# A new VectorE order, gates in long runs, four raw weight blocks and four gathered rows in a dense product-key expert layer

## The chip, the cores and the metric

The kernel runs on one core of a Trainium2 chip. The metric is the device time of one launch in microseconds (us), the median of the runs; lower is better.

## The reference

One inference step of a two-layer decoder for 512 prompt tokens and 8 sample tokens (520 in all, 1024 features, float32). Layer 0 mixes by a recurrence and a latent attention, layer 1 by a convolution module. After each mixer comes the expert layer that this change touches, with 128 x 128 = 16,384 experts, each one row of `u` and one row of `v`:

```python
def block(xb):
    q = (xb @ w_q).reshape(blk, PEER_HEADS, 2, PEER_HALF)          # 8 heads, 2 halves of 128
    s = jnp.einsum('thpd,phkd->thpk', q, sub_keys)
    sv, si = lax.top_k(s, PEER_TOPK)                                # 16 of 128 keys per half
    cand = sv[:, :, 0, :, None] + sv[:, :, 1, None, :]
    cand_idx = si[:, :, 0, :, None] * N_KEYS + si[:, :, 1, None, :]
    top_s, top_pos = lax.top_k(cand.reshape(...), PEER_TOPK)        # 16 experts per head and token
    idx = jnp.take_along_axis(cand_idx.reshape(...), top_pos, axis=-1)
    g = jax.nn.softmax(top_s, axis=-1)
    u, v = u_tab[idx], v_tab[idx]
    act = jax.nn.gelu(jnp.einsum('thkd,td->thk', u, xb), approximate=False)
    return jnp.einsum('thk,thkd->td', g * act, v)
```

The result is added to the scaled input and normalised. Each token picks 128 experts.

## The kernel before

The kernel computes the expert layer densely for most tokens. The experts form 128 blocks of 128. A first pass goes over the blocks of `peer_u` and computes gelu(u x) for all 520 tokens (`hidden` in the code), storing 260 KB a block in HBM (`store`). Beside it the queries are projected, the 16 best keys and pairs are found on VectorE, and for the first TD = 416 tokens a dense matrix of gates is made from one-hot products and stored in HBM by `store_gates`. The other TG = 104 tokens (96 of the prompt and the 8 samples) are gathered: their 128 picks each are fetched row by row.

The second pass, called the output pass here, goes over the 128 blocks of `peer_v`. For block m:

- SyncE loads the raw block into `u` (`load_v`, 512 KB), the hidden values of the 416 tokens into `act` (`load_hid`, 208 KB, four buffers), and for each group of 8 blocks the gates into `g` (`load_gates`, four transfers of 3, 3, 3 and 4 pieces of 128 KB, two buffers).
- ScalarE rounds the raw block to float32r (`high`, L1766, into `uh`, four buffers); it waits for the transfer and for the end of block m-4 on TensorE.
- VectorE forms the remainder (`low`, L1869, into `ul`, four buffers); that frees the raw block. It also makes the product of hidden values and gates (`gated`, L2056, one buffer), its rounded part (`ah`, L2061) and the remainder (`al`, L2063), two buffers each, so that they wait for the end of block m-2 on TensorE. All this is `gate(m, b, par)`.
- TensorE does 24 matmuls of 128x128 by 416 columns (L1731, L1732, L1733 for each of 8 chunks), accumulated in PSUM over all 128 blocks, and counts `block_done`. It waits for `ul` of the block (`split_done`) and `al` (`a_ready`).
- For the gathered tokens GpSimd (POOL) issues, one pick a block, an indirect DMA of one hidden value per token (L1605) and one of one `peer_v` row of 4 KB per token (L1612, 416 KB). They land in a ring of `RING` = 8 buffers. VectorE adds a row to `acc` by L2083 (`add_pick`), LAG = 4 blocks later, and counts `pick_done`.

VectorE's order of block m is `gate(m)`, `low(m+3)`, `add_pick(m-4)`. SyncE's order is `load_v(m+5)`, `load_hid(m+3)`, with the gates of the group after the next between them in the first four blocks of a group. All engines work their instructions in the order in which they are written, with waits on counting semaphores. `u` has two buffers, so `load_v(m)` waits until the remainder of block m-2 is made; the same buffers and waits serve `peer_u` in the first pass.

```python
def load_v(m, b):
    wait(sp, split_done, NK + m - 1)
```

The ring of rows lies over the memory of `xl`, `values` and `ranks`, which the first pass uses; so the first rows are fetched when that pass is done, all of the ring at once.

Of the kernel before, what the change touches and what calls it, by code (L numbers as in the profile page):

```python
# [20 lines left out]
F32 = mybir.dt.float32  # L21
# [7 lines left out]
P = 128  # L29
D = 1024  # L30
# [39 lines left out]
TAIL = ONES + (NP - 1) * PER_TILE + PLAIN + LAST  # L70
RING, LAG = 8, 4
STARTS = tuple(t * TT for t in range(NP)) + (TD,)
SHARES = tuple((NQ * c // 4, NQ * (c + 1) // 4) for c in range(4))
LOW = 3
LOAD = 5
AHEAD = NK
# [26 lines left out]
def wait(eng, sem, value):  # L103

    eng.wait_ge(sem, value)
    if not isinstance(value, int):
        eng.nop(nofuse=True)
# [1232 lines left out]
def peer_experts(nc, k, a, layer, xh, r):  # L1340
# [7 lines left out]
    with Stage(nc, f"experts{layer}") as s:  # L1348
        u = s.sb("u", [P, 2, KC, P])
        uh = s.sb("uh", [P, 4, KC, P], F32R)  # L1350
# [25 lines left out]

        over = Overlay(nc, s, "over_x", 4 * RING * D)
        first = over.row()
# [34 lines left out]
        gates_of = (a["gates"].rearrange("g n j i t -> (g n j i t)")[0:NG * NK * GB * TD]  # L1413
                    .rearrange("(g q j i t) -> g q j i t", g=NG, q=NQ, j=NK, i=GB))
        turn = k.ps[:, 6, 0:3 * TT].rearrange("p (c t) -> p c t", c=3)
# [12 lines left out]
        score_ready = s.sem("score_ready")  # L1428
        landed = [s.sem(f"landed{b}") for b in range(2)]
        high_done = s.sem("high_done")  # L1430
# [32 lines left out]
        with s.block() as block:  # L1463
            @block.sync
            def _(sp):
                def load(n, b):

                    wait(sp, split_done, n - 1)
                    sp.dma_start(u[:, b % 2], a["peer_u"][bass.ds(layer * NK + n, 1)]
                                 .rearrange("o p k e -> (o p) k e")).then_inc(landed[b % 2], 16)  # L1470

                def load_v(m, b):
                    wait(sp, split_done, NK + m - 1)
                    sp.dma_start(u[:, b % 2].rearrange("p k e -> p (k e)"), a["peer_v"][bass.ds(layer * NK + m, 1)]
                                 .rearrange("o e d -> (o e) d")).then_inc(landed[b % 2], 16)

# [5 lines left out]
                def store_gates(piece, par, c):  # L1482

                    n = NG // 4
                    if c == 0:
                        wait(sp, g_free, 2 * PT * piece + 2 * PT + 2)
                    sp.dma_start(gates_of[n * c:n * c + n, bass.ds(piece, 1)].rearrange("g o j i t -> (o j) g (i t)"),
                                 g[:, par, n * GB * c:n * GB * (c + 1)].rearrange("j (g i) t -> j g (i t)", i=GB)
                                 ).then_inc(g_stored[par], 16)

                def load_gates(grp, par, c):

                    q0, q1 = SHARES[c]
                    sp.dma_start(gg[:, par, q0:q1].rearrange("j q i t -> j q (i t)"),
                                 gates_of[bass.ds(grp, 1), q0:q1].rearrange("o q j i t -> (o j) q (i t)")
                                 ).then_inc(g_landed[par], 16)
# [12 lines left out]
                sp.dma_start(keys[:], a["peer_keys"][layer]).then_inc(keys_landed, 16)  # L1509
                sp.dma_start(u[:, 1], a["peer_u"][layer * NK + 1]).then_inc(landed[1], 16)  # L1510
                for n in range(2, LOAD):
                    load(n, n)
# [56 lines left out]
                def out(grp, par, b, last=False):  # L1569

                    m = GB * grp + b
                    if not last or b + LOAD < GB:
                        load_v(m + LOAD, b + LOAD)
                    if not last or b + LOW < GB:
                        load_hid(m + LOW, b + LOW)

# [25 lines left out]
            def _(pool):  # L1602
# [24 lines left out]
                for n in range(RING, P):  # L1627
                    pool.wait_ge(pick_done, n - RING + 1)
                    if n + 8 < P:
                        fetch_hidden(n + 8)  # L1630
                    fetch_row(n)
# [122 lines left out]
            def _(act_e):  # L1754
# [6 lines left out]
                def high(n, b, behind_gelu=False):  # L1761

                    act_e.wait_ge(landed[b % 2], 8 * (n - b % 2) + 16)
                    if not behind_gelu and (not isinstance(n, int) or n >= 4):
                        act_e.wait_ge(block_done, n - 3)
                    act_e.activation(uh[:, b % 4], u[:, b % 2], ACT.Copy).then_inc(high_done, 1)  # L1766

# [92 lines left out]
            def _(v):  # L1860
# [5 lines left out]
                def low(n, b):  # L1866

                    v.wait_ge(high_done, n + 1)
                    v.tensor_tensor(ul[:, b % 4], u[:, b % 2], uh[:, b % 4].bitcast(F32), ALU.subtract).then_inc(split_done, 1)  # L1869

# [176 lines left out]

                def gate(m, b, par):
                    if isinstance(m, int):
                        v.wait_ge(g_landed[par], 64 * (m // (2 * GB)) + 64)  # L2050
                    else:
                        v.wait_ge(g_landed[par], 4 * (m - GB * par - b) + 64)
                    v.wait_ge(hid_landed[b % 4], 4 * (m - b % 4) + 16)
                    if not isinstance(m, int) or m:
                        wait(v, a_ready, m)
                    v.tensor_tensor(gated[:, 0:TD].rearrange("p (q t) -> p q t", q=NQ),  # L2056
                                    act[:, b % 4, 0:TD].rearrange("p (q t) -> p q t", q=NQ),
                                    gg[:, par, 0:NQ, b], ALU.mult).then_inc(gated_ready, 1)
                    v.wait_ge(block_done, NK + m - 1)
                    wait(v, gated_ready, m + 1)  # L2060
                    v.tensor_copy(ah[:, b % 2, 0:TD], gated[:, 0:TD]).then_inc(a_high, 1)  # L2061
                    wait(v, a_high, m + 1)
                    v.tensor_tensor(al[:, b % 2, 0:TD], gated[:, 0:TD], ah[:, b % 2, 0:TD].bitcast(F32), ALU.subtract  # L2063
                                    ).then_inc(a_ready, 1)

                def add_pick(n, b):

                    if b % 8 == 0:
# [3 lines left out]
                        wait(v, weight_made, n + 8)  # L2072
                    v.wait_ge(rows_landed[b % RING], 16 * (n // RING) + 16 if isinstance(n, int) else 2 * (n - b % RING) + 16)
                    row = rows[0:TG, b % RING]
# [13 lines left out]
                def pair(i):  # L2088
                    for par in range(2):
                        for b in range(GB):  # L2090
                            m = 2 * GB * i + GB * par + b
                            gate(m, b, par)
                            if not isinstance(m, int) or m + LOW < NK:
                                low(NK + m + LOW, b + LOW)
                            if not isinstance(m, int) or m >= LAG:
                                add_pick(m - LAG, (GB * par + b - LAG) % 16)

                pair(0)
                with v.Fori(1, NG // 2 - 1) as i:
# [239 lines left out]
```

## Time and profile before

| | us |
|---|---|
| median of 3 runs | 4267.59 (4264.44 to 4269.47) |
| the profiled execution, its own time | 4264.74 |
| its span in the profile | 4262.7 |
| TensorE matmul busy | 3894.4 (91%) |
| VectorE busy | 2679.0 (63%) |
| ScalarE busy | 1169.2 (27%) |
| mean granted clock of TensorE | 0.964 |

The span is the profiled stretch of the one execution that was traced. Busy time of an engine is the time of its instructions, without waiting; matmuls are pipelined, so a busy TensorE isn't TensorE at its peak. The DMA share is the time of all packets over 16 DMA engines; packets of one engine can overlap, so that it can go above 1. A wait is idle time of an engine before an instruction, put down to what came last.

### The profile page before, as it was taken

The numbers are of one execution on the slowest core, as the hardware profiler recorded it, in microseconds if no ns is written. First come the engines' busy times: TensorE is split into PE (matmuls) and PEld (weight loads), VectorE is DVE, ScalarE is ACT, GpSimd is POOL, SyncE is SP. The second block draws the span as 40 slices with busy tenths as digits, with TensorE's granted clock in tenths as the row PEclk, the third lists the DMA queues.
The fourth block names the chain that finished last, engine by engine and source line by source line (L and its number), as shares of the span: only waits on it lengthen the run. The fifth ranks groups of instructions, "written<-read, shape, count | busy, mean of one in ns | idle before, by whom it ended". The sixth has DMA issues, their size and how long they took to land. (4 is left out here: it accounts for less than half of the span.)

```text
span 4262.7 us, 74232 instructions
## 1 busy us (share of the span) xinstructions
PE 3894.4 (91%) x26739; PEld 3653.6 (86%) x26739; DVE 2679.0 (63%) x4909; ACT 1169.2 (27%) x1585; POOL 550.9 (13%) x526
## 2 busy tenths in 40 slices
PE   8887779999999998888888987999999998898997
PEld 8763579999999997888888467999999998888886
DVE  3732256877775246777774846787777424777776
ACT  2211133233333221111113434233333321211212
POOL 0000000000000043333320000000000004333431
PEclk9888889999999999999999988999999999999999
DMA  3137323335445569999962012333554558999994
GB/s 115 50 105 249 124 84 106 119 127 184 157 159 175 187 197 252 258 262 253 258 191 69 20 40 99 107 123 132 175 178 152 184 171 212 253 265 258 268 266 132
DMA packets 342205, 715.74 MB, mean 168 GB/s; under 512 B 43681, under 2 KB 185122, under 8 KB 341666
## 3 DMA queue, kind: packets, MB, share of 16 engines
q1 hardware_dynamic: 296994, 604.61, 45.1%
q0 software_dynamic: 45056, 109.24, 10.6%
q8 instruction: 76, 1.25, 0.1%
q14 instruction: 79, 0.65, 0.1%
HBM read 584.59 MB, written 128.94 MB: 167 GB/s over the span
## 5 line engine op out<-in xcount | busy, mean ns | idle before, releaser
L1667 PE MATMUL ps<-peer_x_then_r_xh,experts_ul 128*128 128x260 f32 x4096 | 1164.2, 284 | 0.0
L1869 DVE TENSOR_TENSOR experts_ul<-experts_u,experts_uh 128x1024 fp32r<-128x1024 f32 x512 | 626.7, 1224 | 848.5 <-ACT experts_uh L1766 836.7
L1668 PE MATMUL ps<-experts_over_x_xl,experts_uh 128*128 128x260 f32 x4096 | 1154.8, 282 | 0.0
L1669 PE MATMUL ps<-peer_x_then_r_xh,experts_uh 128*128 128x260 f32 x4096 | 1153.6, 282 | 0.0
L1731 PE MATMUL ps<-experts_over_a_ah,experts_ul 128*128 128x416 f32 x2048 | 749.2, 366 | 143.7 <-DVE experts_over_a_al L2063 141.9
L1766 ACT ACTIVATE experts_uh<-experts_u 128x1024 fp32r<-128x1024 f32 x512 | 540.4, 1055 | 1081.5 <-PE ps L1733 760.7
L1667 PEld LDWEIGHTS ps<-peer_x_then_r_xh,experts_ul 128*128 128x128 f32 x4096 | 771.8, 188 | 0.0
L1669 PEld LDWEIGHTS ps<-peer_x_then_r_xh,experts_uh 128*128 128x128 f32 x4096 | 770.0, 188 | 0.0
L1668 PEld LDWEIGHTS ps<-experts_over_x_xl,experts_uh 128*128 128x128 f32 x4096 | 769.7, 188 | 0.0
L1732 PE MATMUL ps<-experts_over_a_al,experts_uh 128*128 128x416 f32 x2048 | 727.0, 355 | 0.0
L1733 PE MATMUL ps<-experts_over_a_ah,experts_uh 128*128 128x416 f32 x2048 | 726.1, 355 | 0.0
L1605 POOL DMA_INDIRECT experts_picked<-hidden,experts_h_idx x256 | 278.5, 1088 | 3216.2 <-DMA hidden<-experts_act 1337.3
L1731 PEld LDWEIGHTS ps<-experts_over_a_ah,experts_ul 128*128 128x128 f32 x2048 | 391.7, 191 | 215.1 <-DVE experts_over_a_al L2063 206.6
L1771 ACT ACTIVATE experts_act<-ps 128x520 f32<-128x520 f32 x256 | 154.9, 605 | 1007.1 <-PE ps L1669 1007.0
L1732 PEld LDWEIGHTS ps<-experts_over_a_al,experts_uh 128*128 128x128 f32 x2048 | 392.4, 192 | 2.2
L1733 PEld LDWEIGHTS ps<-experts_over_a_ah,experts_uh 128*128 128x128 f32 x2048 | 391.5, 191 | 2.7
L2083 DVE SCALAR_TENSOR_TENSOR experts_acc<-experts_over_x_rows,experts_weight,experts_acc 104x1024 f32<-104x1024 f32 x254 | 324.9, 1279 | 8.0 <-DVE experts_weight L2071 6.9
L1612 POOL DMA_INDIRECT experts_over_x_rows<-peer_v,experts_v_idx x256 | 262.0, 1023 | 137.2 <-issue 73.4
L1684 PE MATMUL ps<-experts_over_a_onei,experts_over_a_onej 128*128 128x128 f32 x1664 | 203.1, 275 | 9.6 <-DVE experts_over_a_onei L2021 9.6
L1684 PEld LDWEIGHTS ps<-experts_over_a_onei,experts_over_a_onej 128*128 128x128 f32 x1664 | 194.4, 191 | 11.2 <-issue 8.9
L1647 PE MATMUL ps<-peer_x_then_r_xh,experts_over_b_slab_l 128*128 128x260 f32 x512 | 148.6, 290 | 41.8 <-DVE experts_over_x_xl L1876 34.8
L2063 DVE TENSOR_TENSOR experts_over_a_al<-experts_over_a_gated,experts_over_a_ah 128x416 fp32r<-128x416 f32 x256 | 151.6, 592 | 22.2
(356 smaller groups left out, 4950.6 us busy)
## 6 DMA issues: line engine op xcount, KB each, us to landing
experts_u<-peer_u SPq DMA_DIRECT2D x256, 512.0 KB, 3.5
experts_u<-peer_v SPq DMA_DIRECT2D x256, 512.0 KB, 5.9
hidden<-experts_act SPq DMA_DIRECT2D x256, 260.0 KB, 2.1
gates<-experts_over_b_g SPq DMA_DIRECT2D x104, 512.0 KB, 2.9
experts_act<-hidden SPq DMA_DIRECT2D x256, 208.0 KB, 6.2
experts_over_b_g<-gates SPq DMA_DIRECT2D x96, 384.0 KB, 6.6
mla_ct<-cache SPq DMA_DIRECT2D x64, 320.0 KB, 3.9
pa_ct<-cache SPq DMA_DIRECT2D x64, 320.0 KB, 3.9
```

Source lines behind the costliest of these rows:

```text
L1605: pool.indirect_dma_start(out=picked[0:TG, n:n + 1], out_offset=None, in_=a["hidden"].rearrange("n e (t o) -> (n e t) o", o=1), in_offset= ...
L1612: pool.indirect_dma_start(out=rows[0:TG, n % RING], out_offset=None, in_=a["peer_v"].rearrange("i e d -> (i e) d"), in_offset=bass.Indirec ...
L1667: pe.matmul(o, ul[:, b % 4, c], xh[:, c, h, 0:TH], start=(c == 0), stop=False)
L1668: pe.matmul(o, uh[:, b % 4, c], xl[:, c, h, 0:TH], start=False, stop=False)
L1669: mm = pe.matmul(o, uh[:, b % 4, c], xh[:, c, h, 0:TH], start=False, stop=(c == KC - 1))
L1684: mm = pe.matmul(k.ps[:, 4 + m, e * NK:(e + 1) * NK], onej[:, b % 2, 4 * m + e], onei[:, b % 2, 4 * m + e], start=True, stop=True)
L1731: pe.matmul(o, ul[:, b % 4, c], ah[:, b % 2, 0:TD], start=first, stop=False)
L1732: pe.matmul(o, uh[:, b % 4, c], al[:, b % 2, 0:TD], start=False, stop=False)
L1733: mm = pe.matmul(o, uh[:, b % 4, c], ah[:, b % 2, 0:TD], start=False, stop=last)
L1766: act_e.activation(uh[:, b % 4], u[:, b % 2], ACT.Copy).then_inc(high_done, 1)
L1869: v.tensor_tensor(ul[:, b % 4], u[:, b % 2], uh[:, b % 4].bitcast(F32), ALU.subtract).then_inc(split_done, 1)
L2083: v.scalar_tensor_tensor(acc[0:TG], row, w, acc[0:TG], ALU.mult, ALU.add).then_inc(pick_done, 1)
```

## The change

- `u` has four buffers in place of two. `load` and `load_v` wait for the remainder of the block four before, and run LOAD = 7 blocks ahead in place of 5. The first four `peer_u` blocks are asked for at the start.
- The gates lie in HBM as (group, j, piece, i, t) in place of (group, piece, j, i, t). A load now reads, for each of the 128 partitions, one run of 3 or 4 KB in place of 3 or 4 runs of 1 KB; a store still writes runs of 1 KB, which now lie 13 KB apart.
- VectorE's `gate` is cut into `product` (L2056) and `split` (L2061 and L2063). Its order of block m is now `split(m)`, `low(m+2)`, `add_pick(m-4)`, `product(m+1)`.
- SyncE issues `load_hid` ahead of `load_v`.
- `RING` is 4 in place of 8: four rows in the ring, and the hidden values of the picks are asked for after the pick that is four before the row, not eight.

```diff
-RING, LAG = 8, 4
+RING, LAG = 4, 4
-LOAD = 5
+LOAD = 7
...
-        u = s.sb("u", [P, 2, KC, P])
+        u = s.sb("u", [P, 4, KC, P])
...
-        over = Overlay(nc, s, "over_x", 4 * RING * D)
+        over = Overlay(nc, s, "over_x", 4 * KC * 2 * TW + 8 * NT * HP * TOPK)
...
-                    .rearrange("(g q j i t) -> g q j i t", g=NG, q=NQ, j=NK, i=GB))
+                    .rearrange("(g j q i t) -> g j q i t", g=NG, q=NQ, j=NK, i=GB))
...
                 def load_v(m, b):
-                    wait(sp, split_done, NK + m - 1)
-                    sp.dma_start(u[:, b % 2].rearrange("p k e -> p (k e)"), ...
-                                 ).then_inc(landed[b % 2], 16)
+                    wait(sp, split_done, NK + m - 3)
+                    sp.dma_start(u[:, b % 4].rearrange("p k e -> p (k e)"), ...
+                                 ).then_inc(landed[b % 4], 16)
...
-                    sp.dma_start(gates_of[n * c:n * c + n, bass.ds(piece, 1)].rearrange("g o j i t -> (o j) g (i t)"),
+                    sp.dma_start(gates_of[n * c:n * c + n, :, bass.ds(piece, 1)].rearrange("g j o i t -> j g (o i t)"),
...
-                    sp.dma_start(gg[:, par, q0:q1].rearrange("j q i t -> j q (i t)"),
-                                 gates_of[bass.ds(grp, 1), q0:q1].rearrange("o q j i t -> (o j) q (i t)")
+                    sp.dma_start(gg[:, par, q0:q1].rearrange("j q i t -> j (q i t)"),
+                                 gates_of[bass.ds(grp, 1), :, q0:q1].rearrange("o j q i t -> (o j) (q i t)")
...
-                sp.dma_start(u[:, 1], a["peer_u"][layer * NK + 1]).then_inc(landed[1], 16)
-                for n in range(2, LOAD):
+                for n in range(1, 4):
+                    sp.dma_start(u[:, n], a["peer_u"][layer * NK + n]).then_inc(landed[n], 16)
+                for n in range(4, LOAD):
                     load(n, n)
...
                     m = GB * grp + b
+                    if not last or b + LOW < GB:
+                        load_hid(m + LOW, b + LOW)
                     if not last or b + LOAD < GB:
                         load_v(m + LOAD, b + LOAD)
-                    if not last or b + LOW < GB:
-                        load_hid(m + LOW, b + LOW)
...
                     pool.wait_ge(pick_done, n - RING + 1)
-                    if n + 8 < P:
+                    if 16 <= n + 8 < P:
                         fetch_hidden(n + 8)
...
-                def gate(m, b, par):
+                def product(m, b, par):
...
                                     gg[:, par, 0:NQ, b], ALU.mult).then_inc(gated_ready, 1)
+
+                def split(m, b):
                     v.wait_ge(block_done, NK + m - 1)
                     wait(v, gated_ready, m + 1)
...
-                            gate(m, b, par)
-                            if not isinstance(m, int) or m + LOW < NK:
-                                low(NK + m + LOW, b + LOW)
+                            split(m, b)
+                            if not isinstance(m, int) or 0 < m < NK + 1 - LOW:
+                                low(NK + m + LOW - 1, b + LOW - 1)
                             if not isinstance(m, int) or m >= LAG:
                                 add_pick(m - LAG, (GB * par + b - LAG) % 16)
+                            if not isinstance(m, int) or m + 1 < NK:
+                                product(m + 1, (b + 1) % GB, (GB * par + b + 1) // GB % 2)
+
+                product(0, 0, 0)
                 pair(0)
```

## Rows read from the trace of the kernel before

**Rows 1.** Windows of the output pass: busy us (and instructions) by engine, PEclk, DMA share, GB/s.
```profile
...
1560.00:1650.00 90.00, 73.46 (x349) 69.43 (x350) 58.51 (x77) 15.37 (x15) 46.69 (x41) 0.92 0.95 249
1650.00:2150.00 500.00, 446.65 (x2238) 417.46 (x2237) 364.45 (x479) 98.48 (x93) 191.29 (x187) 0.99 0.96 256
3650.00:4150.00 500.00, 454.33 (x2292) 424.18 (x2291) 373.23 (x490) 100.60 (x95) 195.81 (x191) 0.99 0.96 262
...
```

**Rows 2.** The same windows, instructions of line L1731 (TensorE) alone.
```profile
...
1560.00:1650.00 90.00, 44.19 (x117) 23.73 (x117) 0.92 0.95 249
1650.00:2150.00 500.00, 272.03 (x746) 141.69 (x745) 0.99 0.96 256
3650.00:4150.00 500.00, 277.47 (x764) 144.14 (x764) 0.99 0.96 262
...
```

**Rows 3.** Waits in 1650:2150: who for whom, total us, times, longest.
```profile
...
ACT experts_uh L1766 <- PE ps L1733: 251.5, 62, 5.6
ACT experts_uh L1766 <- DMA experts_u<-peer_v: 149.4, 31, 7.8
...
PE ps L1731 <- DVE experts_over_a_al L2063: 53.0, 67, 3.1
...
```

**Rows 4.** Timeline of one block and a half: ScalarE, then VectorE, then TensorE.
```profile
...
1673.97 1.06 ACT L1766 ACTIVATE experts_uh<-experts_u 128x1024 fp32r<-128x1024 f32 x1 [3.46 <-PE ps L1733]
...
1684.09 1.06 ACT L1766 ACTIVATE experts_uh<-experts_u 128x1024 fp32r<-128x1024 f32 x1 [3.55 <-PE ps L1733]
...
1675.06 1.23 DVE L1869 TENSOR_TENSOR experts_ul<-experts_u,experts_uh 128x1024 fp32r<-128x1024 f32 x1 [0.42 <-ACT experts_uh L1766]
1676.20 1.28 DVE L2083 SCALAR_TENSOR_TENSOR experts_acc<-experts_over_x_rows,experts_weight,experts_acc 104x1024 f32<-104x1024 f32 x1
...
1678.56 0.59 DVE L2063 TENSOR_TENSOR experts_over_a_al<-experts_over_a_gated,experts_over_a_ah 128x416 fp32r<-128x416 f32 x1
...
1674.99 0.35 PE L1732 MATMUL ps<-experts_over_a_al,experts_uh 128*128 128x416 f32 x1
...
1679.10 0.35 PE L1733 MATMUL ps<-experts_over_a_ah,experts_uh 128*128 128x416 f32 x1
...
```

**Rows 5.** DMA issues in 1650:2150: count, KB each, median us from issue to landing.
```profile
...
DMA packets 63222, 128.24 MB, mean 256 GB/s; under 512 B 10480, under 2 KB 41583, under 8 KB 63217
...
experts_u<-peer_v SPq DMA_DIRECT2D x93, 512.0 KB, 6.2
experts_act<-hidden SPq DMA_DIRECT2D x94, 208.0 KB, 6.5
...
experts_over_b_g<-gates SPq DMA_DIRECT2D x11, 512.0 KB, 11.0
...
experts_over_x_rows<-peer_v,experts_v_idx POOLq DMA_INDIRECT x93, 7.9
```

**Rows 6.** DMA issues in 1000:1500, the hidden stretch, same columns.
```profile
...
experts_u<-peer_u SPq DMA_DIRECT2D x74, 512.0 KB, 3.6
...
experts_over_b_g<-gates SPq DMA_DIRECT2D x2, 512.0 KB, 3.8
```

**Rows 7.** 10 us windows with DMA share 1.03 or more: first, lowest, highest, last of 36.
```profile
...
1650.00:1660.00 10.00, 8.79 (x47) 8.35 (x46) 5.82 (x10) 1.69 (x2) 4.08 (x4) 1.00 1.05 259
...
1950.00:1960.00 10.00, 8.35 (x44) 7.63 (x42) 7.17 (x11) 1.06 (x1) 2.87 (x3) 1.00 1.04 230
...
2070.00:2080.00 10.00, 9.34 (x48) 8.84 (x48) 7.72 (x11) 2.04 (x3) 4.09 (x4) 1.00 1.05 303
...
4110.00:4120.00 10.00, 9.15 (x49) 8.76 (x48) 7.79 (x10) 2.11 (x2) 4.05 (x5) 1.00 1.03 286
...
```

**Rows 8.** Windows of the hidden stretch and of the pass's start in layer 1.
```profile
...
1100.00:1200.00 100.00, 100.00 (x850) 99.81 (x848) 72.08 (x96) 36.13 (x51) 0.00 (x0) 1.00 0.57 189
...
3560.00:3600.00 40.00, 33.50 (x162) 31.91 (x161) 22.91 (x32) 6.35 (x7) 31.02 (x26) 0.91 1.05 239
...
```

**Rows 9.** Waits of the whole span: ScalarE's for the gate stores.
```profile
...
ACT experts_over_b_g L1783 <- DMA gates<-experts_over_b_g: 35.4, 12, 3.8
...
```

More of the change, by code:

```diff
@@ L1428, in peer_experts @@
         score_ready = s.sem("score_ready")
-        landed = [s.sem(f"landed{b}") for b in range(2)]
+        landed = [s.sem(f"landed{b}") for b in range(4)]
         high_done = s.sem("high_done")
@@ L1466, in load @@
                 def load(n, b):
-                    wait(sp, split_done, n - 1)
-                    sp.dma_start(u[:, b % 2], a["peer_u"][bass.ds(layer * NK + n, 1)]
-                                 .rearrange("o p k e -> (o p) k e")).then_inc(landed[b % 2], 16)
+                    wait(sp, split_done, n - 3)
+                    sp.dma_start(u[:, b % 4], a["peer_u"][bass.ds(layer * NK + n, 1)]
+                                 .rearrange("o p k e -> (o p) k e")).then_inc(landed[b % 4], 16)
                 def load_v(m, b):
-                    wait(sp, split_done, NK + m - 1)
-                    sp.dma_start(u[:, b % 2].rearrange("p k e -> p (k e)"), a["peer_v"][bass.ds(layer * NK + m, 1)]
-                                 .rearrange("o e d -> (o e) d")).then_inc(landed[b % 2], 16)
+                    wait(sp, split_done, NK + m - 3)
+                    sp.dma_start(u[:, b % 4].rearrange("p k e -> p (k e)"), a["peer_v"][bass.ds(layer * NK + m, 1)]
+                                 .rearrange("o e d -> (o e) d")).then_inc(landed[b % 4], 16)
                 def store(n, b):
@@ L1761, in high @@
                 def high(n, b, behind_gelu=False):
-                    act_e.wait_ge(landed[b % 2], 8 * (n - b % 2) + 16)
+                    act_e.wait_ge(landed[b % 4], 4 * (n - b % 4) + 16)
                     if not behind_gelu and (not isinstance(n, int) or n >= 4):
                         act_e.wait_ge(block_done, n - 3)
-                    act_e.activation(uh[:, b % 4], u[:, b % 2], ACT.Copy).then_inc(high_done, 1)
+                    act_e.activation(uh[:, b % 4], u[:, b % 4], ACT.Copy).then_inc(high_done, 1)
                 def gelu(n, b):
@@ L1868, in low @@
                     v.wait_ge(high_done, n + 1)
-                    v.tensor_tensor(ul[:, b % 4], u[:, b % 2], uh[:, b % 4].bitcast(F32), ALU.subtract).then_inc(split_done, 1)
+                    v.tensor_tensor(ul[:, b % 4], u[:, b % 4], uh[:, b % 4].bitcast(F32), ALU.subtract).then_inc(split_done, 1)
                 v.memset(q[:, :, T:NT * TT], 0.0).then_inc(q_cleared, 1)
@@ L2072, in add_pick @@
                         wait(v, weight_made, n + 8)
-                    v.wait_ge(rows_landed[b % RING], 16 * (n // RING) + 16 if isinstance(n, int) else 2 * (n - b % RING) + 16)
+                    v.wait_ge(rows_landed[b % RING], 16 * (n // RING) + 16 if isinstance(n, int) else 16 // RING * (n - b % RING) + 16)
                     row = rows[0:TG, b % RING]
```

## The prediction

> **What bounds the kernel now.** I read the windows first, to see which stretch has room. In the stretches where the hidden values of the experts are computed TensorE is busy all the time (1100 to 1200 us: 100.00 of 100 us) and the DMA engines 0.57 of it [rows 8]; no edit here shortens TensorE's own work, so the diff can gain nothing there. In the output pass (some 690 us in each layer, from 1536 and from 3540 us) TensorE is busy 446.65 and 454.33 of 500 us while the DMA share is 0.96 [rows 1]. This pass is where the change works.
>
> Its pace: a block has 8 matmuls of L1731. 746 of them in 500 us are 93.25 blocks, 5.36 us each; in layer 1, 764 are 95.5 blocks, 5.24 us each [rows 2]. Mean 5.30. What TensorE needs: two matmuls 22 apart start at 1674.99 and 1679.10 us, so one takes 0.187 us and a block of 24 takes 4.49 us [rows 4]. So 0.81 us of each block is lost.
>
> Who makes it wait: in the chain of waits TensorE waits for al (67 times, 53.0 us), al is late because VectorE stood before ul, and ul waits for ScalarE's uh. ScalarE waited 62 times for TensorE (251.5 us) and 31 times for peer_v (149.4 us) [rows 3]. These are two different causes:
>
> First a loop through three engines. high(m+3) may overwrite uh only when block m-1 is done; it starts at 1673.97, then low at 1675.06, the pick at 1676.20, then the product and the cast, and al at 1678.56, which ends at 1679.15: 5.18 us [rows 4]. That frees block m+1, which runs 4.49 us. 9.67 us and the hand-overs make the 10.12 us from that ScalarE activation (1673.97) to the next but one (1684.09): two blocks, 5.06 us each. The loop holds the pace even when every transfer is in time.
>
> Second late transfers. load_v(m+5) is issued after low(m+3), some 2.3 us after TensorE ended block m-1 (1.06 of high, 1.23 of low [rows 4]), and is due when it ends block m+1. That leaves 10.1 - 2.3 = 7.8 us, where the median from issue to landing is 6.2 [rows 5], so the slower ones are late. These are the stalls between 5.06 and 5.30.
>
> **The change part by part.** *VectorE's order.* The same five operations a block, 4.09 us from the start of low to the end of al [rows 4], with a start-up gap some 4.2. Now split(m) comes first and needs only block m-2 done; al is ready about 1.2 us after that, and is needed 4.49 us after it. low(m+2) needs high(m+2), which waits for the same block m-2 and runs beside the split. Low, pick and product end about 4.2 to 4.3 us after it, before block m-1 ends. The 5.06 us loop is gone, and VectorE's own limit, 4.2 to 4.4, lies just under 4.49. Behind the product's wait for hid and gates now stand the next split, low and pick; the split has 3.3 us to spare. Without that cover a late hid costs its whole delay.
>
> *Four raw blocks.* The issue of load_v(m+7) hangs on low(m+3), as load_v(m+5) did, but is due two blocks later: 7.8 us of slack become about 18. It costs no instruction. In the ring of SyncE, load_hid is now issued ahead of load_v; it has about 11 us until its product, against a median landing of 6.5 [rows 5]. The hidden stretches have both the DMA room and a busy TensorE [rows 8], so early u blocks are worth nothing there; I take 0 (at most a few us at each start).
>
> *So the DMA engines are the next limit.* A block moves 512 KB of peer_v, 208 of hidden, 208 of gates and 416 of gathered rows; 128.24 MB over 93.25 blocks is 1.375 MB [rows 2, 5]. What can they give when they never run dry? From one side: of the 100 windows of 10 us in 1650:2150 and 3650:4150, 36 have a share of 1.03 or more (packets overlap, so it passes 1), with a mean of 274 GB/s, lowest 230 [rows 7]. That is 5.01 us a block. From the other side: the engine time of a block is 0.96 x 5.30 = 5.09 us [rows 1, 2]; at the 1.045 that the full windows show, 4.87 us. The first picks out the windows heavy in gathered rows, the second takes packets to grow no slower under load. I take 4.94, the middle.
>
> *Gates in long runs.* Loads of 1 KB runs become runs of 3 to 4 KB. In the uncrowded stretch 512 KB of gates take 3.8 us to land where 512 KB of peer_u take 3.6: 5%. In the output pass it is 11.0 against 6.2 for peer_v, 44% [rows 5, 6]. At 257 GB/s 208 KB are 0.83 us, so the bounds are 0.04 and 0.36 us a block; part of the 11.0 is the queue ahead of it, so I take the nearer 0.04: 4.90 us. A loss is not excluded either: 128 write runs of the store now lie 13 KB apart. Stores land in the stretch with free DMA and the two buffers of g hide them; I take 0, and at most the 35.4 us that ScalarE waits for stores today could double [rows 9].
>
> *Four gathered rows.* A row is asked for after the pick four earlier, not eight: POOL takes about 2.4 us to issue the pair, then 7.9 median to land [rows 5], against four blocks, 19.6 us. Hidden, and only a landing over 17 us would show. At the start four rows fewer, 1.70 MB, go ahead of the first peer_v blocks, in a window of 249 GB/s where a block takes 90 / (117 / 8) = 6.2 us [rows 1, 2]: 6.8 us a layer. Two more blocks are loaded before the pass, where the DMA has room: 1.05 MB, 4 us. That is 0 to 22 us in both layers; rows put off come back as load, so I take 13.
>
> Sum: from 1650 us to the last loads some 102 blocks a layer, 204 x (5.30 - 4.90) = 82 us, and 13: 95. The profiled execution took 4264.7 us (span 4262.7), so 4170; the median of the runs is 2.9 above that execution, so **4173 us**.
>
> One page of the Trainium skill makes another case of it. The rows show 1.04 of share with 274 GB/s. DMA: Bandwidth & Descriptors, "Where 436 GB/s comes from", gives some 358 GB/s as what HBM lets a core have, and more when it is alone. At 358, 1.375 MB would be 3.8 us and TensorE's 4.49 the bound, as in the second rival. In this pass the trace does not agree: no full 10 us window passes 303.
>
> The opposite is in HBM Reference, "Latency": an access takes 0.2 us on average and 2 us at high load. By that, more loads under way buy waiting and not rate, as in the third and the last rival. The trace agrees in part: peer_u lands in 3.6 us in the quiet stretch and peer_v in 6.2 here.
>
> **The rivals.** *Forecast, 0.52:* the DMA engines set 4.8 to 5.0 us, 4150 to 4195.
>
> *TensorE becomes the bound, 0.18.* If the contention between gathered rows and the rest eases once both are spread evenly, or long runs bring the 0.36, the pace is 4.6 with the clock's dips: 204 x 0.70 = 143, and the some 29 blocks of the two starts (2 x 117 / 8) go from 6.2 to about 5.1, 32 us. 175 us: 4093. At 4.49 throughout, 204 x 0.81 + 32 = 197: 4070. For it: 303 GB/s in one window would carry 4.54. Against: share 0.96 already.
>
> *Only a part comes, 0.16.* The rate does not rise above today's in full windows of layer 0, 270 GB/s, and late hid or gates take the place of late peer_v: 5.1 to 5.2 us. 204 x 0.15 = 31: about 4237.
>
> *Nothing, 0.06.* The loop was a shadow of a DMA bound that holds today: 5.30 stays, 4268.
>
> *Slower, 0.08: rate lost to more transfers at once.* When eight rows and the peer_v loads go together at the start of layer 1, the share is 1.05 and only 239 GB/s move [rows 8]. With four raw blocks always under way that could be the lasting state: 1.375 / 0.239 = 5.75 us, 204 x 0.45 = 92 us more, 4360. It decides below 1.375 / 5.30 = 259 GB/s. For it: 23 full windows of layer 0 lie only 12 GB/s above that on the mean. Against: the rows come one a block either way, and the start has eight of them at once.
>
> **How the numbers follow.** The likeliest case gives 4173. The slower side of the part case ends near 4245, the TensorE case reaches to about 4080; this range leaves out the no-change and slower cases (0.14) and the far edge of TensorE's (0.04). What this kernel's measurement can tell from no change is about 0.2%, 8.5 us. Faster 0.86, same 0.06, slower 0.08.
>
> **What would show it.** ScalarE's waits for peer_v nearly vanish (31 in layer 0's 500 us); about 102 blocks (816 of L1731) in 1650:2150 in place of 93.25; DMA share above 1.00 in most 10 us windows, at 265 to 285 GB/s; VectorE waits at the product for hidden or gates, or at the split for TensorE. TensorE idle next to a DMA share under 0.95 would mean a new wait, hid first, then rows. A rate under 259 at a share of 1.04 would make the prediction wrong in sign; TensorE busy all through at over 290 GB/s, wrong in size.

## The result, and the profile after

The changed kernel takes 4231.38 us in the median (4227.86 to 4243.52), the kernel before 4266.01 us in the runs beside it. The ratio is 0.9924, 95% interval [0.9905, 0.9943]: 0.76% faster, some 32 us where 95 were forecast. The time lies in the stated range, near the value of the third case ("only a part comes", 4237). The profiled execution took 4235.68 us, with a span of 4233.6.

TensorE's matmuls of the output pass run from 1531.7 to 2204.9 us and from 3520.5 to 4193.8 us: 673.2 and 673.3 us, where they took 689.7 (1536.4 to 2226.1) and 683.9 us (3540.3 to 4224.2). That is 27 us of the 29 by which the two spans differ.

The windows of the pass after, as in [rows 1] (busy us and instructions of TensorE, its weight loads, VectorE, ScalarE, POOL; clock, DMA share, GB/s), and under them those of L1732 alone, which is L1731 of before:

```profile
...
1560.00:1650.00 90.00, 80.21 (x396) 77.31 (x396) 66.31 (x89) 17.32 (x17) 47.88 (x37) 0.94 0.97 263
1650.00:2150.00 500.00, 450.75 (x2279) 435.18 (x2278) 366.97 (x485) 101.40 (x96) 223.42 (x190) 0.97 1.00 260
3650.00:4150.00 500.00, 448.43 (x2257) 433.22 (x2256) 364.76 (x482) 99.57 (x94) 227.52 (x188) 0.96 0.99 260
...
1560.00:1650.00 90.00, 48.55 (x132) 26.13 (x132) 0.94 0.97 263
1650.00:2150.00 500.00, 275.19 (x760) 146.72 (x760) 0.97 1.00 260
3650.00:4150.00 500.00, 273.59 (x753) 146.06 (x752) 0.96 0.99 260
...
```

760 and 753 of L1732 are 95.0 and 94.1 blocks in 500 us: 5.26 and 5.31 us a block, mean 5.29, against 5.30 before [rows 2]. The steady pace did not move; 102 blocks were forecast. The DMA share rose from 0.96 to 1.00 and 0.99, but the rate stayed at 260 GB/s (256 and 262 before).

Only the start of the pass is better. These are the first 90 us of the pass in each layer, the same line alone, before and after:

```profile
...
1536.40:1626.40 90.00, 45.24 (x120) 24.16 (x120) 0.92 0.87 227
3540.30:3630.30 90.00, 45.07 (x117) 24.19 (x117) 0.89 0.88 222
...
1531.70:1621.70 90.00, 49.88 (x139) 26.42 (x139) 0.98 0.88 236
3520.50:3610.50 90.00, 50.10 (x138) 26.80 (x139) 0.96 0.86 235
...
```

That is 19 and 21 matmuls of this line more, 5 blocks in both layers; at 5.3 us a block they are 26 of the 27 us.

The chain of waits in 1650:2150 (who for whom: total us, times, longest), as [rows 3]:

```profile
...
ACT experts_uh L1767 <- PE ps L1734: 408.5, 96, 11.3
...
DVE experts_over_a_gated L2057 <- issue: 54.3, 28, 4.9
DVE experts_over_a_gated L2057 <- DMA experts_act<-hidden: 52.5, 24, 5.3
PE ps L1732 <- DVE experts_over_a_al L2066: 48.9, 29, 5.0
...
```

ScalarE's 31 waits for peer_v are gone. In their place VectorE waits 52 times at the product, 24 times with the hidden values named, for 106.8 us in all; where "issue" is named, the profile shows no releaser. TensorE waits 29 times for 48.9 us, where it waited 67 times for 53.0: fewer and longer stalls, the same sum. DMA issues (count, KB each, median us to landing), as [rows 5]:

```profile
...
DMA packets 50534, 130.01 MB, mean 260 GB/s; under 512 B 10537, under 2 KB 22545, under 8 KB 50530
...
experts_u<-peer_v SPq DMA_DIRECT2D x94, 512.0 KB, 9.4
experts_act<-hidden SPq DMA_DIRECT2D x94, 208.0 KB, 11.7
...
experts_over_x_rows<-peer_v,experts_v_idx POOLq DMA_INDIRECT x95, 10.4
```

peer_v lands after 9.4 us in place of 6.2, the hidden values after 11.7 in place of 6.5: more is under way at the same rate, so everything is under way longer. The 11.7 us are more than the 11 us that the prediction gave load_hid.

Between stalls the new order does what it should. ScalarE's activations of three blocks in a row (start, length, line, what ended the idle time):

```profile
...
1672.04 1.06 ACT L1767 ACTIVATE experts_uh<-experts_u 128x1024 fp32r<-128x1024 f32 x1 [3.42 <-PE ps L1734]
1676.58 1.06 ACT L1767 ACTIVATE experts_uh<-experts_u 128x1024 fp32r<-128x1024 f32 x1 [3.48 <-PE ps L1734]
1681.00 1.06 ACT L1767 ACTIVATE experts_uh<-experts_u 128x1024 fp32r<-128x1024 f32 x1 [3.36 <-PE ps L1734]
1685.47 1.06 ACT L1767 ACTIVATE experts_uh<-experts_u 128x1024 fp32r<-128x1024 f32 x1 [3.42 <-PE ps L1734]
1692.21 1.06 ACT L1767 ACTIVATE experts_uh<-experts_u 128x1024 fp32r<-128x1024 f32 x1 [5.68 <-PE ps L1734]
...
```

1685.47 - 1672.04 is 13.43 us for three blocks, 4.48 each, TensorE's own pace; the fourth takes 6.74, the stall. So the kernel has a fast pace and stops for data. The question is why the DMA engines, at a share of 1.00, move no more than 260 GB/s.

### The profile page after: what moved, and what is told of

Read it like the earlier page. It is cut to its first block and busy times, and to the rows that moved or that the text cites. A ratio compares the mean times of both kernels' runs of the same rounds, so it can differ in the third digit from the quotient of the medians.

```text
span 4233.6 us, 74185 instructions
## 1 busy us (share of the span) xinstructions
PE 3878.6 (92%) x26739; PEld 3673.4 (87%) x26739; DVE 2674.5 (63%) x4909; ACT 1171.3 (28%) x1585; POOL 630.8 (15%) x526
## 5 line engine op out<-in xcount | busy, mean ns | idle before, releaser
L1732 PE MATMUL ps<-experts_over_a_ah,experts_ul 128*128 128x416 f32 x2048 | 743.3, 363 | 130.4 <-DVE experts_over_a_al L2066 130.0
L1732 PEld LDWEIGHTS ps<-experts_over_a_ah,experts_ul 128*128 128x128 f32 x2048 | 396.8, 194 | 163.8 <-DVE experts_over_a_al L2066 159.3
L1613 POOL DMA_INDIRECT experts_over_x_rows<-peer_v,experts_v_idx x256 | 342.4, 1337 | 121.4 <-issue 73.6
L2057 DVE TENSOR_TENSOR experts_over_a_gated<-experts_act,experts_over_b_g 128x416 f32<-128x416 f32 x256 | 150.9, 589 | 264.5 <-DMA experts_act<-hidden 134.1
```

Of the source, the lines that this page charges most:

```text
L1613: pool.indirect_dma_start(out=rows[0:TG, n % RING], out_offset=None, in_=a["peer_v"].rearrange("i e d -> (i e) d"), in_offset=bass.Indirec ...
L1732: pe.matmul(o, ul[:, b % 4, c], ah[:, b % 2, 0:TD], start=first, stop=False)
```

## The experiments

In each table of this section the ratio is to the kernel before, run on the same chip, with its 95% interval; blocks are the matmuls of `ah` with `ul` (L1731 before, L1732 after) in 1650:2050 over 8 (before 599 / 8 = 74.9, after 615 / 8 = 76.9), and GB/s is that window's rate (258 and 261).

### What in the transfers sets the rate

Three theories: 1, a ceiling on bytes at 260 GB/s; 2, the gathered rows slow the rest (by their scattered addresses, by the software queue, or otherwise); 3, there is rate to spare and only the hidden values stand in the wrong place.

`e1_rows_plain_pool` replaces the gather:

```diff
-                    pool.indirect_dma_start(
-                        out=rows[0:TG, n % RING], out_offset=None, in_=a["peer_v"].rearrange("i e d -> (i e) d"),
-                        in_offset=bass.IndirectOffsetOnAxis(ap=v_idx[0:TG, n:n + 1], axis=0),
-                    ).then_inc(rows_landed[n % RING], 16)
+                    pool.dma_start(rows[0:TG, n % RING], a["peer_v"][layer * NK + n, 0:TG]).then_inc(rows_landed[n % RING], 16)
```

> The changed kernel, but the 104 rows of a pick are 104 neighbouring rows of peer_v, loaded by a plain transfer on GpSimd's queue: same bytes, same software queue, no scattered addresses (the picked rows are replaced, so the gathered tokens get other rows). Theory 1, a ceiling on bytes (the pass moves about 260 GB/s whatever the transfers are): the pace of a block stays at 5.28 us, the time within 10 us of the changed kernel. Theory 2, scattered rows are what is slow: rate 290 to 330 GB/s, pace 4.6 to 4.8 us, 120 to 170 us faster. Theory 3, hidden values come late because they stand behind peer_v in SyncE's ring: no change, as in theory 1, but with DMA share left over.

`e2_rows_plain_sync` has the same plain rows in SyncE's `out`, behind `load_v`:

```diff
...
+                    sp.dma_start(rows[0:TG, b % RING], a["peer_v"][bass.ds(layer * NK + m, 1), 0:TG].rearrange("o e d -> (o e) d")
+                                 ).then_inc(rows_landed[b % RING], 16)
...
```

> As the run before, but the plain rows are issued on SyncE's queue after load_v, so that in the pass the software queue carries only the 4-byte hidden values (rows replaced as there). Theory 1: pace 5.28 us, rate 260 GB/s still. Theory 2, if it is the second queue and not the addresses that slows the packets: rate 300 or more, pace at TensorE's 4.5 to 4.7 us, 150 us faster. Theory 3: one more transfer a block ahead of the hidden values in the same ring, so slower, 5.4 us or more.

`e3_no_gate_loads` puts a count in place of the transfer in `refill`:

```diff
-                    load_gates(grp + 2, par, c)
+                    sp.sem_inc(g_landed[par], 16)
```

> The changed kernel without the gate loads after the first two groups of a layer (the gates of the first two groups are used again): 1.163 MB a block in place of 1.376. Theory 1: 1.163 MB at 260 GB/s is 4.47 us, so TensorE's 4.49 us becomes the bound, pace 4.5 to 4.65 us, 160 to 190 us faster, DMA share about 0.95. Theory 2: the rows and what runs beside them cost what they did, 4.5 to 4.7 us as well. Theory 3: hidden values still stand behind four peer_v blocks, pace 5.0 to 5.2 us, at most 60 us faster.

`e4_64_gathered` is the one line `TD = 448`.

> The changed kernel with TD = 448 in place of 416, which is 64 gathered prompt tokens in place of 96: 72 rows in place of 104 a pick (288 KB), hidden and gates 224 KB each, 1.278 MB a block; TensorE's block is 448/416 of 4.49, 4.83 us; some 18 us more for the gate matmuls of 32 more tokens in both layers. Theory 1: 1.278 MB at 260 GB/s is 4.92 us, 92 us less and 18 more: 4155 to 4165 us. Theory 2: fewer rows lift the rate too, TensorE is the bound at 4.85 to 4.9 us: 4140 to 4150 us. Theory 3: 5.2 us, about 4240 us.

| run | us | ratio | blocks | GB/s |
|---|---|---|---|---|
| e1_rows_plain_pool | 4120.70 | 0.9651 [0.9622, 0.9680] | 82.8 | 286 |
| e2_rows_plain_sync | 4229.77 | 0.9898 [0.9847, 0.9950] | 74.8 | 255 |
| e3_no_gate_loads | 4139.08 | 0.9692 [0.9662, 0.9722] | 81.6 | 238 |
| e4_64_gathered | 4162.42 | 0.9755 [0.9722, 0.9787] | 82.0 | 262 |

Theory 3 falls with e3: without the gate loads, 15% fewer bytes, the kernel is 92 us faster than the changed one, where theory 3 allowed 60. Theory 1 falls too: the same bytes in e1 move at 286 GB/s, and in e3, with the rows' part of the bytes larger, at 238; its pace is 400 / 81.6 = 4.90 us where a ceiling of 260 GB/s gave 4.5 to 4.65. So the rows are suspect. e4 with fewer of them came out as theory 1 said (4155 to 4165), but does not tell the two apart: its pace is 400 / 82.0 = 4.88 us and TensorE's block there is 4.83. Theory 2 in the forms asked for doesn't fit either: e3 is slower than the 4.5 to 4.7 us it gave, and away from the software queue (e2) the rows were as slow as before.

### The addresses, or the number of rows

`g1_indirect_neighbours` leaves the indirect transfers and overwrites their list:

```diff
-                v.tensor_scalar(v_idx[:], pair_of[:], float(layer * NK * P), None, ALU.add)
+                v.tensor_scalar(number[:], k.iota[:], float(P), token[:], ALU.mult, ALU.add).then_inc(idx_made, 1)
+                v.wait_ge(idx_made, 3)
+                v.tensor_scalar(v_idx[:], number[:], float(layer * NK * P), None, ALU.add)
...
```

> The changed kernel with its indirect transfers of rows as they are, but the list of addresses is overwritten by 104 neighbouring rows of peer_v a pick (so other rows than the picked ones are added). Theory 2a, scattered addresses are what costs: as with plain rows on GpSimd's queue, pace 4.8 to 4.85 us, 284 to 290 GB/s, about 4120 us. Theory 2b, the indirect form of transfer costs (how its 104 descriptors are made and spread over the engines): pace stays at 5.2 to 5.3 us, about 4230 us.

`g2_112_rows` gathers eight rows more, which no one reads:

```diff
-                        out=rows[0:TG, n % RING], ...
-                        in_offset=bass.IndirectOffsetOnAxis(ap=v_idx[0:TG, n:n + 1], axis=0),
+                        out=rows[0:112, n % RING], ...
+                        in_offset=bass.IndirectOffsetOnAxis(ap=v_idx[0:112, n:n + 1], axis=0),
```

> The changed kernel, gathering 112 rows a pick in place of 104 (the last 8 are not used; 104 isn't divisible by 16, 112 is). Theory 2a, scattered rows cost by their number: 8% more rows, pace 5.35 to 5.45 us, 15 to 35 us slower than the changed kernel. Theory 2c, 104 rows are spread unevenly over the 16 DMA engines and that costs the rate: share and rate rise, pace under 5.1 us, 40 us or more faster.

`s4_128_rows` and `q3_120_rows` are the same edit with 128 and 120, `r1_96_rows` with 96 after the first four picks, and `r2_128_plain_sync` is e2 with 128 plain rows.

> The changed kernel, gathering 128 rows a pick (the last 24 unused): 1.474 MB a block in place of 1.376, but 8 rows for each of 16 engines. If the even spread is what 112 rows brought: the engines give some 309 GB/s, 4.77 us a block, 4105 to 4140 us, faster than 104 rows although 7% more bytes move. If the busiest engine counts alone (8 rows either way, as with 13 engines of 8 rows): 4230 us or more.

> The changed kernel, gathering 120 rows a pick (120 = 15 x 8). Theory 4 in its exact form, the number of engines that take part is the largest divisor up to 16: 15 engines of 8 rows, between 104 (13 of 8, 4231 us) and 128 (16 of 8, 4055 us): 4060 to 4130 us. If only a multiple of 16 matters: 4240 us or more, by the 15% more rows.

> The changed kernel, gathering 96 rows (16 x 6) a pick after the first four picks (the 8 sample tokens keep the rows of the first four, so their result is left out). 120 rows were no faster than 104, so sharing by a divisor up to 16 is not all of it. If a multiple of 16 is what counts, 96 are at least as fast as 128: 4045 to 4070 us. If each engine must write its own 8 partitions (128 fits, 112 nearly, 96 least), rows stay slow: 4120 us or more, slower than 112 rows though fewer bytes.

> As e2_rows_plain_sync (plain rows on SyncE's queue, other rows than the picked ones) but 128 rows of it in place of 104. If the row count alone made that run slow: as fast as 128 gathered rows, 4050 to 4070 us. If plain rows on SyncE's queue are slow for another reason (one ring for all): 4230 us or more, with 7% more bytes.

| run | rows | us | ratio | blocks | GB/s |
|---|---|---|---|---|---|
| r1_96_rows | 96 | 4054.99 | 0.9490 [0.9463, 0.9518] | 88.3 | 296 |
| g1_indirect_neighbours | 104 | 4235.53 | 0.9914 [0.9890, 0.9939] | 75.8 | 258 |
| g2_112_rows | 112 | 4067.03 | 0.9541 [0.9507, 0.9576] | 87.8 | 309 |
| q3_120_rows | 120 | 4239.10 | 0.9936 [0.9911, 0.9960] | 74.9 | 267 |
| s4_128_rows | 128 | 4055.13 | 0.9498 [0.9478, 0.9518] | 88.5 | 326 |
| r2_128_plain_sync | 128, plain | 4037.64 | 0.9449 [0.9422, 0.9476] | 88.6 | 327 |

Neighbouring addresses in the same indirect transfer change nothing (4235.53). Eight rows more make the kernel 164 us faster than the changed one. The 128-row kernels came out faster than was expected of them. Windows in 1650:2050, one row each of 104 rows (after), 112, 120 and 128:

```profile
...
1650.00:2050.00 400.00, 363.76 (x1846) 352.32 (x1845) 295.40 (x389) 82.33 (x78) 181.42 (x154) 0.97 1.00 261
...
1650.00:2050.00 400.00, 396.70 (x2106) 393.44 (x2105) 340.26 (x449) 92.94 (x88) 211.21 (x175) 1.00 1.02 309
...
1650.00:2050.00 400.00, 359.52 (x1795) 349.62 (x1794) 291.23 (x383) 78.48 (x74) 182.28 (x150) 0.94 1.00 267
...
1650.00:2050.00 400.00, 400.00 (x2125) 397.63 (x2125) 346.64 (x455) 94.29 (x89) 196.37 (x178) 1.00 0.92 326
...
```

The two shares of 1.00 in the uneven cases stand for 261 and 267 GB/s; with 128 rows a share of 0.92 stands for 326, and TensorE is busy 400.00 of 400 us. TensorE's granted clock (0.97 after, 1.00 with 128 rows) is 3% apart and cannot make paces of 5.20 and 4.52 us a block, 15% apart. The DMA issues of the same four (packets and rate, peer_v, rows):

```profile
...
DMA packets 40643, 104.44 MB, mean 261 GB/s; under 512 B 8492, under 2 KB 18173, under 8 KB 40640
...
experts_u<-peer_v SPq DMA_DIRECT2D x76, 512.0 KB, 9.1
...
experts_over_x_rows<-peer_v,experts_v_idx POOLq DMA_INDIRECT x77, 10.3
...
DMA packets 45590, 123.72 MB, mean 309 GB/s; under 512 B 7698, under 2 KB 18902, under 8 KB 45586
...
experts_u<-peer_v SPq DMA_DIRECT2D x88, 512.0 KB, 6.5
...
experts_over_x_rows<-peer_v,experts_v_idx POOLq DMA_INDIRECT x88, 8.1
...
DMA packets 39720, 106.96 MB, mean 267 GB/s; under 512 B 7114, under 2 KB 16620, under 8 KB 39717
...
experts_u<-peer_v SPq DMA_DIRECT2D x75, 512.0 KB, 8.9
...
experts_over_x_rows<-peer_v,experts_v_idx POOLq DMA_INDIRECT x75, 10.6
...
DMA packets 47376, 130.43 MB, mean 326 GB/s; under 512 B 7784, under 2 KB 19093, under 8 KB 47372
...
experts_u<-peer_v SPq DMA_DIRECT2D x88, 512.0 KB, 5.2
...
experts_over_x_rows<-peer_v,experts_v_idx POOLq DMA_INDIRECT x89, 6.2
```

With 128 rows both the rows and peer_v, which nobody touched, land in little more than half the time of after, though a row transfer is 23% larger. SyncE's queue (hardware_dynamic in the profile) carries the same transfers a block in all of these kernels. Packets, MB and the share of 16 engines that its packets took, with 104, 112 and 128 rows:

```profile
...
q1 hardware_dynamic: 27278, 72.02, 65.7%
...
q1 hardware_dynamic: 31546, 83.30, 65.6%
...
q1 hardware_dynamic: 31767, 83.83, 58.0%
...
```

Over 76.9, 87.8 and 88.5 blocks these are 3.42, 2.99 and 2.62 us of engine time a block for the same bytes: the other transfers' packets last longer beside 104 rows, at a full share too (after and 112).

96, 112 and 128 rows are fast, 104 and 120 slow. What separates the five is that the number of partitions is a multiple of 16. 120 rows were expected to lie between 104 and 128 if only the number of engines that take part mattered; they were as slow as 104. r1 speaks against each engine having to write its own eight partitions. r2 shows the same on the other queue: e2 was slow by its 104 rows, and 128 rows there are the fastest run of all.

Two runs limit the rule. The 72 rows of e4 are no multiple of 16 either, and its TensorE was busy 399.02 of 400 us: it needed only 262 GB/s, so it can't show whether 72 rows are slow. And the transfers of one hidden value a token kept their 104 partitions in every run of the table, the fast ones too; with 4 bytes a partition they did not hold the rate down.

The Trainium skill, DMA: Bandwidth & Descriptors, "Why a DMA increments its semaphore by 16 and not by 1", says that a transfer runs on the largest number of engines up to 16 that divides the slowest dimension of both its sides, here the rows, and names one exception: the software queue spreads some plain transfers over all 16, the partitions over 16 rounded up on each. By that, 96, 112 and 128 rows run on 16, 104 on 13 and 120 on 15, and e1, if it is such an exception, puts 7 rows on an engine and fills 15. The split into fast and slow agrees with it. e1's 104 rows (286 GB/s) lie between the gathered 104 (261) and 112 (309), yet gathered rows on 15 engines (q3) gave 267. So the time does not follow from counting engines, and the page doesn't say why 15 cost as much as 13.

### What the parts of the change are worth

With 104 rows: `p1_gates_short` undoes the layout of the gates, `q1_104_rows_old_order` and `q2_104_rows_two_raw` undo the order and the raw blocks, `p2_before_ring4` is the kernel before with the ring alone. With 112 rows: `s1_before_112_rows`, `s2_112_rows_old_order`, `s3_112_rows_two_raw`. The edits of order and raw blocks are those of the diff of the change, taken back; their main lines:

```diff
-                            split(m, b)
-                            if not isinstance(m, int) or 0 < m < NK + 1 - LOW:
-                                low(NK + m + LOW - 1, b + LOW - 1)
+                            product(m, b, par)
+                            split(m, b)
+                            if not isinstance(m, int) or m + LOW < NK:
+                                low(NK + m + LOW, b + LOW)
...
-                            if not isinstance(m, int) or m + 1 < NK:
-                                product(m + 1, (b + 1) % GB, (GB * par + b + 1) // GB % 2)
-
-                product(0, 0, 0)
...
```

```diff
-LOAD = 7
+LOAD = 5
...
-        u = s.sb("u", [P, 4, KC, P])
+        u = s.sb("u", [P, 2, KC, P])
...
-                    wait(sp, split_done, NK + m - 3)
+                    wait(sp, split_done, NK + m - 1)
...
```

> The changed kernel with the layout of the gates of before (loads in 1 KB runs). If the runs are worth what the prediction took, 0.04 us a block, 8 to 10 us slower than the changed kernel, about 4240 us; if engine time sets the pace (a packet of 1 KB costs more for its bytes than one of 3 KB), up to 0.36 us a block and 4300 us; under a bound by scattered rows no change, 4230 us.

> The kernel before with only the ring of rows cut from 8 to 4. If the gain of the change lies in the starts of the two passes and comes from the four rows that no longer go ahead of the first peer_v blocks: 10 to 14 us a layer faster than before, about 4240 us. If it comes from the four raw blocks or the order: no change, 4266 us. If the ring of 8 hid late rows: slower than before.

> The changed kernel (104 rows) with VectorE's order of before. If the 35 us of the change come from the order: 4260 to 4270 us. Theory 4, the uneven rows hold both orders at 5.2 to 5.3 us a block and the loop of 5.06 is covered by them: within 10 us of 4231 us.

> The changed kernel (104 rows) with two raw blocks and LOAD 5. If the four raw blocks brought the 35 us, since under a slow rate the late peer_v blocks need the longer lead: 4255 to 4270 us. If the order brought them, with peer_v late but nothing queued behind it on VectorE that TensorE needs at once: 4230 to 4240 us.

> The kernel before, gathering 112 rows a pick in place of 104. Theory 4: today both kernels are held by the uneven spread of 104 rows over the DMA engines; with that gone the kernel before meets its next limit, the loop of high, low, pick, product and split with TensorE, 5.06 us a block: passes of some 650 us, 4190 to 4215 us. If the loop were no limit of its own: as fast as the changed kernel with 112 rows, 4067 us.

> The changed kernel with 112 rows and VectorE's order of before (product, split, low(m+3), pick), everything else as changed. Theory 4: the loop is back, 5.06 us a block where transfers are in time, 4185 to 4205 us. If the order is worth nothing: 4067 us.

> The changed kernel with 112 rows and two raw weight blocks (LOAD 5) in place of four, VectorE's new order kept. A peer_v block has some 6.9 us between its issue and its need, against a landing of 6.5 us median: late about every other time, pace 4.7 to 4.9 us, 4100 to 4150 us. If the raw blocks are worth nothing: 4067 us.

| run | us | ratio | blocks | GB/s |
|---|---|---|---|---|
| p1_gates_short | 4231.46 | 0.9917 [0.9886, 0.9948] | 76.1 | 260 |
| p2_before_ring4 | 4284.10 | 1.0033 [1.0012, 1.0054] | 73.5 | 253 |
| q1_104_rows_old_order | 4298.48 | 1.0070 [1.0050, 1.0090] | 71.9 | 247 |
| q2_104_rows_two_raw | 4230.62 | 0.9916 [0.9898, 0.9933] | 75.6 | 259 |
| s1_before_112_rows | 4209.05 | 0.9867 [0.9844, 0.9889] | 78.0 | 274 |
| s2_112_rows_old_order | 4180.03 | 0.9794 [0.9772, 0.9817] | 78.6 | 278 |
| s3_112_rows_two_raw | 4087.14 | 0.9581 [0.9554, 0.9609] | 87.3 | 307 |

With even rows the loop of the prediction comes out. The kernel before with 112 rows paces 400 / 78.0 = 5.13 us and the changed one with the old order 400 / 78.6 = 5.09, where the loop was put at 5.06; with the new order it is 4.56 (g2). What waits in s2 and in s3:

```profile
...
ACT experts_uh L1767 <- PE ps L1734: 319.3, 79, 5.0
...
DVE experts_ul L1870 <- ACT experts_uh L1767: 75.3, 69, 1.9
...
PE ps L1732 <- DVE experts_over_a_al L2066: 34.7, 39, 1.2
...
ACT experts_uh L1767 <- DMA experts_u<-peer_v: 268.8, 75, 6.7
...
PE ps L1732 <- DVE experts_over_a_al L2066: 4.9, 6, 1.1
```

In s2 no wait for a transfer is left, and TensorE still waits 39 times for al: the loop by itself. In s3 ScalarE waits 75 times for peer_v, but in the new order nothing that TensorE needs at once stands behind it, and TensorE waits six times for 4.9 us. So the late peer_v blocks, which the prediction took for a cause of their own, cost little once the order is new: 20 us between s3 and g2, nothing with 104 rows (q2 is level with the changed kernel). s3 came out faster than was expected of it; q1 fell outside both of its expectations on the slow side.

## Why the prediction was right in its case for a gain and wrong in its size

The step that failed is "So the DMA engines are the next limit". It read the share of 0.96 as room: 274 GB/s from full windows, 4.87 us from engine time, and between them 4.94 us a block. But with 104 rows the transfers already held the pace near 5.3 us: 112 rows alone make the kernel before 1.3% faster (s1). Measured: the share of 1.00 and 0.99 in the two layers, mean 0.995, times 5.29 is 5.26 us of engine time a block, where 5.09 was held fixed; the packets of a block took 3% longer in all. So the share rose without the rate. Full windows were no measure of the rate either: of the changed kernel's in 1650:2150 the fastest and the slowest with a share of 1.03 or more are

```profile
...
1920.00:1930.00 10.00, 10.00 (x55) 9.94 (x54) 7.30 (x10) 2.12 (x2) 3.12 (x4) 1.00 1.05 298
...
2120.00:2130.00 10.00, 8.71 (x45) 7.97 (x43) 5.79 (x8) 1.27 (x3) 3.93 (x4) 1.00 1.03 222
...
```

and the mean over 500 us is still 260. The time of a packet is no measure of what the engines could do: with 128 rows a block of 7% more bytes took 0.92 x 4.52 = 4.16 us of engine time. The 82 us of the steady stretch were 204 x (5.30 - 5.29) = 2, and the 13 us of the two starts were some 26. That 104 rows set this limit is shown by g2, s4 and r1; by what mechanism uneven rows do it stays open.

Point by point, the rest:

- **The loop** of 5.06 us a block was real, but the rows' limit lay over it, at 5.3. Freed from them it measured 5.13 (s1) and 5.09 (s2). With 104 rows the order is worth more than the whole change: without it the changed kernel is 0.7% slower than before, with it 0.76% faster. In that run (q1) the pace is 400 / 71.9 = 5.56 us at 247 GB/s and a share of 1.01, and peer_v lands after 13.9 us; why was not tried further.
- **VectorE's limit** of 4.2 to 4.4 us under TensorE's 4.49 held: with 128 rows TensorE never stops and the pace is 400 / 88.5 = 4.52.
- **Four raw blocks**: the waits for peer_v vanished, as forecast, and the time didn't change; the stalls moved to the product and its hidden values, which were named as the next to be late. With two raw blocks and the new order (q2) peer_v lands after 6.8 us at 259 GB/s, with four (after, same window) after 9.1 at 261: the longer landing is the queue, not a slower rate.
- **Long gates**: 0.04 us a block was taken; nothing measurable (4231.46 against 4231.38), and no loss from the stores.
- **Four rows in the ring**: no late rows in the steady stretch, as forecast. The ring does bring the start: in 1560:1650 the line has 117 matmuls before, 129 with the ring alone (p2), 131 without the new order (q1), 130 without the raw blocks (q2) and 132 with everything. So the 13 us of the sum were too small, not too large. But alone the ring makes the kernel 0.33% slower, since the steady stretch has 588 matmuls in 400 us against 599. The 1.70 MB a layer that are put off are some 6.5 us at 260 GB/s; that they explain it was not shown.
- **The rivals**: "only a part comes" hit the time (4237 against 4231) by luck. It had the late hidden values and the unchanged rate right, but its 31 us were to come from a steady pace of 5.1 to 5.2 us, which stayed at 5.29, while the starts brought what it did not count. For the steady stretch the rival given 0.06, "nothing", was right: a bound by the DMA that held before too. The low rate of the last rival (239 GB/s) did not become the lasting state, but q1 comes close to it: four raw blocks with the old order, 247 GB/s, below the 259 that it named, and slower than before. TensorE as the bound was right about the kernel and wrong about this change: it needed eight more rows. The Trainium skill's 358 GB/s (DMA: Bandwidth & Descriptors, "Where 436 GB/s comes from") is not contradicted after all: 327 GB/s were reached at a share of 0.91 with TensorE the bound (r2), and one window of 10 us with 128 rows (s4, 1910:1920) shows 401. The Trainium skill's statement that HBM accesses take longer at high load (HBM Reference, "Latency") agrees with landings that grew from 6.2 to 9.4 us at the same rate with more loads under way, but load by itself is not the cause: with 128 rows more bytes move and peer_v lands after 5.2.

The version to keep is the changed kernel with 128 gathered rows, the result unchanged: 4055.13 us, 5.0% faster than before.

## What to carry to other kernels

A DMA share near 1 says that packets are under way all the time, not that the engines give what they can; compare the rate with that of another stretch or shape before taking it for the limit. Where a large transfer, gathered or plain, has a number of partitions that 16 does not divide, try one that it does, padded with rows that nobody reads: 23% more bytes in the gather were 176 us faster. And a part of a change is worth something only against the limit that binds: the same new order was worth 67 us with 104 rows and 113 with 112, the raw blocks 0 and 20.

## What was not expected of the hardware

- In the changed kernel's order and with all its loads, gathered rows of 4 KB, 104 or 120 a block, and 104 plain ones on SyncE's queue hold the core at 255 to 267 GB/s at a share of 0.94 to 1.01; with 96, 112 and 128 rows it is 296 to 327, limited by TensorE. Neighbouring addresses changed nothing. The form matters on GpSimd's queue: 104 plain rows there gave 286 GB/s (e1).
- One uneven row transfer slows the others: peer_v, 128 partitions throughout, landed after 9.1 us beside 104 rows, 6.5 beside 112 and 5.2 beside 128.
- 15% more rows (120) keep nearly the pace of 104: 599 and 615 matmuls of L1732 in 400 us. What makes 15 of 16 as dear as 13 of 16 stays open; no view shows which engine carried what.
